# A mixture-of-experts layer on one core: prompt rows first in the experts' down product and in the last stage

## The reference, cut to what is computed

```python
def expert_choice_ffn(h, w_router, w_gate, w_up, w_down):
    cap = CAPACITY_FACTOR * T // N_EXPERTS
    aff = jax.nn.softmax((xf @ w_router).astype(jnp.float32), axis=-1)
    g, idx = lax.top_k(aff.T, cap)
    xs = xf[idx]
    hid = jax.nn.silu(jnp.einsum('ecd,edf->ecf', xs, w_gate)) * jnp.einsum('ecd,edf->ecf', xs, w_up)
    ys = jnp.einsum('ecf,efd->ecd', hid, w_down) * g[..., None].astype(h.dtype)
    out = jnp.zeros((T, D), h.dtype).at[idx.reshape(-1)].add(ys.reshape(-1, D))
...
    return x + gt2 * rms_norm(y, p['norm_post_ffn'][l])
```

## Time and profile before

| | |
|---|---|
| time, median of 3 executions | 3544.34 us (3540.55 to 3546.19) |
| the profiled execution's own time | 3544.65 us |
| its span from the first to the last instruction | 3542.6 us |
| TensorE busy | 3339.1 us, 94% of the span |
| VectorE, ScalarE, GpSimd busy | 2157.0, 1611.4, 627.4 us |
| mean granted TensorE clock | 0.973 of full speed |

### The profile page before, as it was taken

The page is one execution under the profiler, slowest core; times in us unless marked ns, Lnnn a source line. Parts: engine busy times, 40 slices in busy tenths (PEclk is TensorE's granted clock), DMA queues, the critical chain, the costliest instruction groups (busy, mean ns, idle before and its releaser), DMA issues. The chain is left out here.

```text
span 3542.6 us, 58031 instructions
## 1 busy us (share of the span) xinstructions
PE 3339.1 (94%) x21806; PEld 2828.2 (80%) x21806; DVE 2157.0 (61%) x4031; ACT 1611.4 (45%) x2475; POOL 627.4 (18%) x802
## 2 busy tenths in 40 slices
PE   7999999999999999899999399999999999999992
PEld 5777777677778778787777299999999999999991
DVE  3655555454688888565555665555655566555556
ACT  3656666453444453454544144444444444444443
POOL 1111101341122222043233101111111111111102
PEclk9999999999999999999999599999999999999996
DMA  7444444556555545666665545555555555555577
GB/s 235 165 134 153 151 149 151 167 186 191 177 181 164 156 149 155 186 228 200 207 207 179 224 137 170 172 172 172 172 172 172 167 166 170 172 172 170 165 253 283
DMA packets 540690, 633.06 MB, mean 179 GB/s; under 512 B 82432, under 2 KB 421984, under 8 KB 540512
## 3 DMA queue, kind: packets, MB, share of 16 engines
q1 hardware_dynamic: 492624, 484.73, 42.8%
q0 software_dynamic: 41024, 135.33, 12.0%
q10 hardware_dynamic: 6864, 10.60, 0.8%
HBM read 504.72 MB, written 125.86 MB: 178 GB/s over the span
## 5 line engine op out<-in xcount | busy, mean ns | idle before, releaser
L2899 DVE TENSOR_TENSOR moe_w_lo<-c_w_raw,moe_w_hi 128x2048 fp32r<-128x2048 f32 x192 | 439.9, 2291 | 365.5 <-ACT moe_w_hi L2830 365.2
L111 PE MATMUL moe_pg<-c_parts,moe_w_hi 128*128 128x320 f32 x2048 | 633.8, 309 | 1.8 <-DVE c_parts L2937 1.8
L113 PE MATMUL moe_pg<-c_parts,moe_w_lo 128*128 128x320 f32 x2048 | 632.4, 309 | 0.0
L112 PE MATMUL moe_pg<-c_parts,moe_w_hi 128*128 128x320 f32 x2048 | 632.3, 309 | 0.0
L2830 ACT CAST moe_w_hi<-c_w_raw 128x2048 fp32r<-128x2048 f32 x192 | 364.6, 1899 | 86.2 <-PE moe_pd L3072 73.0
L111 PEld LDWEIGHTS moe_pg<-c_parts,moe_w_hi 128*128 128x128 f32 x2048 | 384.5, 188 | 3.0 <-issue 2.2
L112 PEld LDWEIGHTS moe_pg<-c_parts,moe_w_hi 128*128 128x128 f32 x2048 | 384.4, 188 | 0.6
L113 PEld LDWEIGHTS moe_pg<-c_parts,moe_w_lo 128*128 128x128 f32 x2048 | 384.4, 188 | 0.0
L111 PE MATMUL gla_pd<-c_parts,gla_w_hi 128*128 128x512 f32 x640 | 260.1, 406 | 7.8 <-DVE gla_w_lo L1224 3.9
L113 PE MATMUL gla_pd<-c_parts,gla_w_lo 128*128 128x512 f32 x640 | 253.5, 396 | 0.0
L112 PE MATMUL gla_pd<-c_parts,gla_w_hi 128*128 128x512 f32 x640 | 251.8, 393 | 0.0
(11 more groups left out here) (409 smaller groups left out, 7350.5 us busy)
## 6 DMA issues: line engine op xcount, KB each, us to landing
c_w_raw<-in_w_gate_e_dram SPq DMA_DIRECT2D x64, 1024.0 KB, 4.7
c_w_raw<-in_w_up_e_dram SPq DMA_DIRECT2D x64, 1024.0 KB, 4.7
c_w_raw<-in_w_down_e_dram SPq DMA_DIRECT2D x64, 1024.0 KB, 4.9
c_w_raw<-in_w_in_dram SPq DMA_DIRECT2D x80, 512.0 KB, 3.9
c_w_raw<-in_w_in_dram SPq DMA_DIRECT2D x35, 1024.0 KB
scratch_gate<-gla_sg POOLq DMA_DIRECT2D x80, 256.0 KB, 2.7
mix_sg<-scratch_gate SPq DMA_DIRECT2D x40, 512.0 KB, 5.7
c_h_raw<-scratch_hT SPq DMA_DIRECT2D x33, 512.0 KB, 7.2
```

The lines of the kernel that those rows point to most:

```text
L111: pe.matmul(out, w_hi, x_hi, start=start, stop=False)
L112: pe.matmul(out, w_hi, x_lo, start=False, stop=False)
L113: return pe.matmul(out, w_lo, x_hi, start=False, stop=stop)
L2899: dve.tensor_tensor(w_lo[:, m % 2], w_raw[:, m % 2], w_hi[:, m % 2].bitcast(F32), ALU.subtract).then_inc(s_wlo, 1)
```

## The change

The order of the three row tiles becomes 2, 0, 1: the prompt rows first, then the two sample tiles. It is changed at four places together: TensorE's loop over the tiles in chunks 8 to 11, ScalarE's evictions, the counts that both wait for, and GpSimd's scatters. The last stage begins with the four prompt tiles: SyncE waits for the first tile of the last chunk and for the prompt's scatter before the first four loads, and for the rest before the fifth. The buffers of the last stage are numbered anew, so that the first four tiles go to the buffers of chunk 10's weights (the halves with index 0). VectorE's code is not touched.

```diff
-        ORDER = list(range(NP, NT)) + list(range(NP))
+        ORDER = list(range(NT))
+        ROW_ORDER = (2, 0, 1)
...
-            return tile_of((w_hi[:].bitcast(F32), w_lo[:].bitcast(F32)), n % NY)
+            return tile_of((w_hi[:].bitcast(F32), w_lo[:].bitcast(F32)), (0, 1, 4, 5, 2, 3, 6, 7)[n % NY])
...
-                sp.wait_ge(s_d, N_EXP * 6)
-                sp.wait_ge(K.sample_added, 32)
+                sp.wait_ge(s_d, N_EXP * 6 - 2)
+                sp.wait_ge(K.prompt_added, 16)
                 for n, t in enumerate(ORDER):
-                    if n == NT - NP:
-                        sp.wait_ge(K.prompt_added, 16)
+                    if n == NP:
+                        sp.wait_ge(s_d, N_EXP * 6)
+                        sp.wait_ge(K.sample_added, 32)
...
-                    for r in range(3):
-                        pool.wait_ge(s_de, e * 6 + 3 + r + 1)
+                    for i, r in enumerate(ROW_ORDER):
+                        pool.wait_ge(s_de, e * 6 + 3 + i + 1)
...
-                            for r in range(3):
+                            for i, r in enumerate(ROW_ORDER):
                                 h = (m - 8) // 2
                                 act.wait_ge(s_gn, e + 1)
-                                act.wait_ge(s_d, e * 6 + h * 3 + r + 1)
+                                act.wait_ge(s_d, e * 6 + h * 3 + i + 1)
...
-                            for r in range(3):
+                            for i, r in enumerate(ROW_ORDER):
                                 if g == 0:
-                                    wait(pe, s_de, e * 6 + h * 3 + r - 2)
+                                    wait(pe, s_de, e * 6 + h * 3 + i - 2)
```

## The result

| | before | changed |
|---|---|---|
| time, median of 4 executions | 3543.49 us (3540.55 to 3546.19) | 3628.75 us (3622.82 to 3630.82) |
| profiled execution, span | 3542.6 us | 3629.1 us |
| mean granted clock | 0.973 | 0.959 |

The ratio is 1.0236, 95% interval 1.0223 to 1.0248: 2.4% slower, against 3626.9 us predicted (3600 to 3640).

The account below looks back on a forecast made before the run. The experts' stage was taken as bound by TensorE, so any added wait adds time: 3544.65 + 49.1 (pause) + 36.0 (clock) − 2.8 (last stage) = 3626.9 us, 2.3% slower, range 3600 to 3640.

Parts of the forecast that it names:

- The wait that takes the place of the old one: Start of chunk 10: TensorE waits 3.70 us for the prompt rows' scaled copy; net 3.27 us per expert, 49.1 us.
- the old wait before chunk 11: TensorE's wait for the low halves of chunk 11's weights, 0.43 us in each of 15 experts, predicted to go away.
- The clock: Chunk 10 after the pause: matmuls run slow at 1.2 GHz, 2.4 us per expert, 36.0 us; bounds 0 and 2.5.
- one price for each of 15 experts: Chunk 10 after the pause: the lowered clock was costed at 2.4 us in every one of 15 experts.
- The clock holds: Rival, chunk 10: the pause comes but TensorE stays at 2.4 GHz in nearly all experts; 3591 us, chance 0.12.
- No pause: Rival, chunk 10: the scaled copy ends before TensorE leaves the transposes, so nothing waits; 3535 us, chance 0.04.
- A longer slow spell: Rival, experts: the clock falls a second time in an expert, costing 4 to 5 us; 3658 us, chance 0.04.
- slow spells that show in the slices: Sign: granted clock 0.50 for some 5 us after the pause in each of 15 experts, visible in the page's slices.
- The last stage: After the experts: prompt loads go out 3.1 us earlier, the first sample tile starts sooner; gain 2.8 us, bounds 0 and 4.0.
- a last stage that takes longer: Sign, after the experts: a longer last stage would show the prediction wrong; it had claimed a gain of 2.8 us.
- their mutual slowing: Last stage: prompt loads and the two sample scatters slow each other by 2.8 us, leaving no gain.
- After it VectorE paces the stage as now: Last stage, after the first sample tile: VectorE sets the pace as before, 16 tiles either way.

Follow-up runs that it names:

- second set: The changed kernel, unedited, run again beside the kernel with only the row order changed: 3625.15 us (4 runs), ratio 1.0213.

## Why the prediction was right, and where it was off

*The wait that takes the place of the old one.* Right in place, cause and size: 15 pauses of 3.70 us, and the addition decides them. Moved, they are gone; moved half way, they shrink to 2.31 us. The net was 3.12 us rather than 3.27, because what the old wait before chunk 11 cost was worth 0.58 us an expert (89.90 − 89.32), not the 0.43 that I took from the late matmul alone.

*The clock.* Right in size: keeping TensorE at work in the pause takes 36.8 us off the changed kernel's first median and 33.2 us off that of its second set, and I had 36.0. In the first profiled run the clock cost 2.56 us an expert, just above my upper bound of 2.5. The step that was too simple is one price for each of 15 experts: the prices are 0, 1.63 and 2.56 us, and which one is paid changes within a run and between runs. That the sum came out at 5.67 against 5.68 us an expert owes something to two opposite errors of about 0.15 us, and to a profiled run in which every expert paid the full price.

*The rivals.* "The clock holds" was priced at 3591 us, and the kernel with busy pauses took 3592. As a forecast it was wrong for the changed kernel's runs, but it is what 6 of 14 experts did in the two profiled runs of the row order alone. The Trainium skill (TensorE: Matmul & The Clock Gate, "HAM oscillation — how this bites in real kernels") describes idle gaps in a loop that let the clock fall in each pass. The first profiled run agrees, with a fall in 14 of 14 experts; the others do not. After waits of 3.45 us, which lie above the page's limit for a gap, it fell in 8 or 11 of 14, and after waits of 2.0 us, below it, in 6 of 14. The prediction read that limit as leaning to a clock that holds; the waits here are above it, so by the page the clock would fall in every pass. "No pause" was priced at 3535 us with VectorE's addition as its condition; with that condition met the kernel took 3536. A longer slow spell was seen in no profiled run. One sign that I had named, slow spells that show in the slices, could not come: they are too short for slices of 91 us.

*The last stage.* This term was mis-sized: 2.8 us predicted, 0.3 measured in the first profiled run, and from a loss of 1.3 to a gain of 1.0 us over the six profiled runs with the new last stage, with a mean of nothing. So the lower bound of 0 was too high, and a last stage that takes longer, which I had named as a sign of being wrong, is in the record. The step that failed is the one that carried the loads' and scatters' times over unchanged: 5.5 us from the first load to the first tile (measured 8.4) and 7.4 us for the last sample scatter to land (measured 11.3). I had named their mutual slowing as the lower bound and should have taken it, since the change itself makes them overlap. A third figure erred the other way: I allowed 12.4 us from the first sample load to the fifth tile, and it took 10.5 (3585.62 − 3575.11), so that tile was only 1.5 us later than predicted. The prompt scatter went out 1.1 us earlier than I had worked out, 2.5 us before TensorE's end; the slow loads took that too. "After it VectorE paces the stage as now" failed by the new pause of 1.0 us.

## What to carry to other kernels

When the order of work on one engine moves a consumer forward, look at where its producer stands in the program of every other engine: here one addition of 0.67 us, left behind eight operations that had nothing to do with it, cost some 90 us, and moving it is worth 0.3% over the kernel before under either order. A pause of a busy TensorE has two prices, its length and the slow matmuls behind it; they can be told apart by filling the pause with matmuls nobody needs. A transfer that is started earlier meets whatever still runs then, so its duration is not to be copied from a trace in which it ran alone.

## What the runs showed of the hardware

Equal pauses of 3.45 us, in one program, cost 0, 1.63 or 2.56 us of granted clock, so the same kernel took 3602.5 to 3633.6 us over its eight executions, while the kernel with the pauses filled stayed within 3590.5 to 3595.1. Beside two accumulating scatters of 128 rows each, the first tile came 7.6 to 8.7 us after its load was issued in six profiled runs; beside scatters of 2 rows it came after 5.6 us, and where the loads were issued after the sample scatters had landed, after 5.5 us.
